# Hybrid decoder step on one core: in prompt attention TensorE does the value products and the turn back ahead of the next group's logits

## The chip, the core and the metric

The kernel runs on one core of a Trainium2 chip. The metric is the device time of one execution in microseconds (us), the median of several runs. Five engines work side by side, each through its own queue of instructions in program order, and meet by semaphores: TensorE (PE, its weight loads listed apart as PEld), VectorE (DVE), ScalarE (ACT), GpSimd (POOL) and SyncE (SP, which issues DMAs).

## What is computed

One decoder layer over a prompt of 2048 positions and a decode batch of 64 positions with a paged cache. Projection, forgetting attention and pooling, output mix and norm, then a convolutional feed-forward block with norm. The change touches only the prompt's attention, 8 heads of width 64, in float32:

```python
s = jnp.einsum('bqhd,bkhd->bhqk', q, k).astype(jnp.float32) * ATTN_SCALE
s = s + jnp.swapaxes(qc, 1, 2)[..., :, None] - jnp.swapaxes(kc, 1, 2)[..., None, :]
s = jnp.where(causal, s, NEG_INF)
p = jax.nn.softmax(s, axis=-1)
return jnp.einsum('bhqk,bkhd->bqhd', p.astype(v.dtype), v)
```

## The kernel before

The stages follow one another: `stage_project`, `stage_gates_pool`, `stage_attention`, `stage_mix_prompt`, then feed-forward with the decode batch's attention beside it. The prompt attention is `stage_attention`.

**Groups, steps and pairs.** The work is cut into 32 groups: a head and a block of 512 queries (four rows r of 128 queries). The blocks of a head are taken 0 to 3, those of the next head 3 to 0. Group g of a head sees 4g+4 blocks of 128 keys, and each of these is a step: 320 steps, done two at a time in 160 pairs. In this text p is a pair, and p-1 the one before it.

**What a pair holds.** Six kinds of work, with a letter for each that the prediction uses:

- T(p), TensorE, `transposes`, L912: the exponentials of the pair's two key blocks, up to 8 tiles of 128x128, are turned into a bank of `ps_t` for each step. There are four banks (TBANKS); a bank is free when DVE has read it (`t_free`).
- H(p), ACT, `high`, L1029: the rounded upper half of each bank goes to `p_hi`.
- R(p), DVE, `rest`, L977: what is left, bank minus `p_hi`, goes to `p_lo`, and frees the bank. DVE does R(p-1) in its turn of pair p.
- V(p), TensorE, `times_v`, L924 and L926: two products with the values for each step, summed in `ps_o`. V(p-1) is done in TensorE's turn of pair p, and waits for R(p-1) by `t_free`.
- L(p), TensorE, `logits`, L896, L897 and, where a piece has the diagonal, L900: pieces of up to 512 logits of the *next* group, in three banks of `ps_s` (SBANKS). A table, `logits_at`, spreads the 320 pieces over the pairs by columns: 115 pairs have some (one to eight pieces), 45 have none, those at the end of a group.
- C(p), DVE, `copy_logits`, L965 (with a small reduce, L969, after a row's last piece): scales the piece into `row`, takes its minimum and frees its bank.

Besides these ACT does the exponentials (`exp`, L1021) by the table `exps_at` and, at a group's end, copies `ps_o` out (`o_out`, L1035). In the second pair of the next group TensorE turns that copy back (`turn_back`, L936, four matmuls into a `ps_t` bank), and in the pair after it DVE normalises it (`normalise`, L984, L987, L994).

**What sets the order.** Each engine's program is written out by hand as a loop over pairs. TensorE's is T(p), L(p), V(p-1), turn back. DVE's is

```python
if 1 <= pair <= PAIRS:
    rest(i - 2)
    rest(i - 1)
for n in nat_at.get(pair - 1, []):
    normalise(n)
for n, r, j in logits_at.get(i, []) + logits_at.get(i + 1, []):
    copy_logits(n, r, j)
```

so it is R(p-1), the normalising where there is one, C(p). ACT's is H(p), the copy out, the exponentials. The numbers of `ps_t` banks (`tick_of`, `nat_tick`) are set by a loop of their own, which the change leaves alone.

Of the kernel before, what the change touches and what calls it, by code (L numbers as in the profile page):

```python
# [757 lines left out]
def stage_attention(nc, io, sc, persist):  # L758
    groups = [(h, g) for h in range(H) for g in (range(4) if h % 2 == 0 else reversed(range(4)))]
    NGR = len(groups)  # L760
    steps = [4 * g + 4 for _, g in groups]
    first_t = [sum(steps[:n]) for n in range(NGR + 1)]
    NTR = first_t[NGR]
# [10 lines left out]
    def pieces(n, r):  # L774
        return cut(n, r, PIECE)
# [20 lines left out]
    logits_at, exps_at = {}, {}  # L796
# [41 lines left out]
    with ExitStack() as ctx:  # L838
# [44 lines left out]
        def _(pe):  # L883
            def logits(n, r, j):
                h, g = groups[n]
                par, q = h % 2, 4 * g + r
                if n % 4 == 0 and r == 0:
                    pe.wait_ge(head_in[par], 128 * (h // 2 + 1))
                cols = slice(q * P, (q + 1) * P)
                o, w = pieces(n, r)[j]  # L890
                p = piece_of[n, r] + j
                if p >= SBANKS:
                    pe.wait_ge(s_copied, p - SBANKS + 1)
                out, keys = ps_s[:, p % SBANKS, 0:w], slice(o, o + w)
                diagonal = keys.stop == (q + 1) * P
                nc.tensor.matmul(out, qs[:, par, cols], ks[:, par, keys], start=True, stop=False, skip_group_check=True)  # L896
                last = nc.tensor.matmul(out, q2[:, par, cols], k2[:, par, keys], start=False, stop=not diagonal,  # L897
                                        skip_group_check=True)
                if diagonal:
                    last = nc.tensor.matmul(out[:, w - P:w], identb[:, :], causal[:, :], start=False, stop=True,  # L900
                                            skip_group_check=True)
                last.then_inc(s_done, 1)

            def transposes(i):
                n, k = turns[i]
                tk = tick_of[i]
                if k * P % HALF == 0:
                    pe.wait_ge(exp_done, exps_until(n, k * P // HALF))
                if tk >= TBANKS:
                    pe.wait_ge(t_free, tk - TBANKS + 1)  # L910
                for r in range(skip(i), 4):
                    last = nc.tensor.transpose(ps_t[:, tk % TBANKS, r * P:(r + 1) * P],  # L912
                                               row[:, n % 2, r, k * P:(k + 1) * P], ident[:, :])
                last.then_inc(t_done, 1)

            def times_v(i):
                n, k = turns[i]
                h, o = groups[n][0], skip(i) * P
                pe.wait_ge(t_free, tick_of[i] + 1)
                if n % 4 == 0 and k == 0:  # L920
                    pe.wait_ge(v_in[h % 2], 16 * (h // 2 + 1))
                if k == 0 and n:
                    pe.wait_ge(o_copied, n)
                nc.tensor.matmul(ps_o[:, o:512], v[:, h % 2, k, :], p_hi[:, i % PBUF, o:512], start=k == 0, stop=False,  # L924
                                 skip_group_check=True)
                nc.tensor.matmul(ps_o[:, o:512], v[:, h % 2, k, :], p_lo[:, i % PBUF, o:512], start=False,  # L926
                                 stop=k == steps[n] - 1, skip_group_check=True).then_inc(pv_done, 1)

            def turn_back(n):
                tk = nat_tick[n]  # L930
                if n == 0:
                    pe.wait_ge(c_in, 32)
                pe.wait_ge(o_copied, n + 1)
                pe.wait_ge(t_free, tk - TBANKS + 1)
                for r in range(4):
                    last = nc.tensor.matmul(ps_t[:, tk % TBANKS, r * HD:(r + 1) * HD], oT[:, n % 2, r * P:(r + 1) * P], both[:, :],  # L936
                                            start=True, stop=True)
                last.then_inc(nat_done, 1)
# [3 lines left out]
            for pair in range(PAIRS + 2):  # L942
                i = 2 * pair
                if pair < PAIRS:
                    transposes(i)
                    transposes(i + 1)
                    for n, r, j in logits_at.get(i, []) + logits_at.get(i + 1, []):
                        logits(n, r, j)
                if 1 <= pair <= PAIRS:
                    times_v(i - 2)  # L950
                    times_v(i - 1)
                for n in nat_at.get(pair, []):
                    turn_back(n)

        @block.vector
        def _(dve):
# [1691 lines left out]
```

## Time and profile before

| | us |
|---|---|
| median of 3 runs | 3067.35 |
| lowest and highest | 3066.34, 3074.68 |
| the profiled execution, its own time | 3075.47 |
| span of its trace | 3073.8 |
| attention stage in it, from 462 to 947 | 485.0 |

Over the whole span PE is busy 2939.5 us (96%), DVE 2009.4 (65%), ACT 1484.3 (48%), POOL 811.1 (26%). These are averages over stages with different limits; for the change the stage between 462 and 947 us is to be read by itself. The views print, for a stretch, each engine's busy time and the granted clock of TensorE (PEclk, 1.00 is 2.4 GHz and 0.50 is 1.2 GHz); in the timeline an instruction's start, its length, and in brackets how long its engine was idle before it and who released it. Lengths of matmuls hold a modelled end, so matmuls overlap in the list; the distance from start to start is what one costs TensorE.

### The profile page before, as it was taken

The numbers are of one execution on the slowest core, as the hardware profiler recorded it, in microseconds if no ns is written. First come the engines' busy times: TensorE is split into PE (matmuls) and PEld (weight loads), VectorE is DVE, ScalarE is ACT, GpSimd is POOL, SyncE is SP. The second block draws the span as 40 slices with busy tenths as digits, with TensorE's granted clock in tenths as the row PEclk, the third lists the DMA queues.
The fourth block names the chain that finished last, engine by engine and source line by source line (L and its number), as shares of the span: only waits on it lengthen the run. The fifth ranks groups of instructions, "written<-read, shape, count | busy, mean of one in ns | idle before, by whom it ended". The sixth has DMA issues, their size and how long they took to land. (4 is left out here: it accounts for less than half of the span.)

```text
span 3073.8 us, 56650 instructions
## 1 busy us (share of the span) xinstructions
PE 2939.5 (96%) x19248; PEld 2367.9 (77%) x19248; DVE 2009.4 (65%) x4190; ACT 1484.3 (48%) x3057; POOL 811.1 (26%) x1437
## 2 busy tenths in 40 slices
PE   7999968999998997999999999999999999999997
PEld 7999957777777885877777777777777777777762
DVE  5433447787786656866678667678667668666454
ACT  3111115676674213466445656445665435666424
POOL 1110010000000103534445333455344353342300
PEclk9999978999999998999999999999999999999999
DMA  5444465224203447767979677888677886775877
GB/s 208 137 138 123 117 170 129 70 56 97 77 1 131 131 144 241 254 202 241 310 258 314 225 238 246 282 300 296 212 254 241 273 302 226 250 250 169 288 273 322
DMA packets 271943, 629.62 MB, mean 205 GB/s; under 512 B 53400, under 2 KB 117816, under 8 KB 263680
## 3 DMA queue, kind: packets, MB, share of 16 engines
q1 hardware_dynamic: 171095, 308.46, 31.4%
q0 software_dynamic: 93760, 296.83, 29.1%
q10 hardware_dynamic: 6800, 20.71, 2.1%
q8 instruction: 154, 2.52, 0.3%
q14 instruction: 134, 1.09, 0.1%
HBM read 558.66 MB, written 67.33 MB: 204 GB/s over the span
## 5 line engine op out<-in xcount | busy, mean ns | idle before, releaser
L1615 PE MATMUL F_ps_u<-X_x_hi,F_w_hi 128*128 128x512 f32 x1408 | 572.9, 407 | 7.0 <-DVE F_w_lo L1879 7.0
L1616 PE MATMUL F_ps_u<-X_x_lo,F_w_hi 128*128 128x512 f32 x1408 | 560.3, 398 | 0.0
L1617 PE MATMUL F_ps_u<-X_x_hi,F_w_lo 128*128 128x512 f32 x1408 | 560.1, 398 | 0.0
L2157 POOL DMA_DIRECT2D N_dec<-cache_v x512 | 282.0, 551 | 618.9 <-PE F_ps_d L1679 484.7
L1879 DVE TENSOR_TENSOR F_w_lo<-X_raw,F_w_hi 128x512 fp32r<-128x512 f32 x352 | 238.1, 678 | 239.5 <-ACT F_w_hi L1777 238.4
L2117 POOL DMA_DIRECT2D N_dec<-cache_k x512 | 278.1, 543 | 338.5 <-issue 188.3
L1938 DVE STREAM_TRANSPOSE N_dec<-N_dec 128x1024 f32<-128x1024 f32 x256 | 310.5, 1230 | 49.2 <-DMA N_dec<-cache_k 49.2
L1777 ACT CAST F_w_hi<-X_raw 128x512 fp32r<-128x512 f32 x352 | 215.7, 613 | 251.9 <-PE F_ps_y L1617 200.4
L1615 PEld LDWEIGHTS F_ps_u<-X_x_hi,F_w_hi 128*128 128x128 f32 x1408 | 266.8, 190 | 85.5 <-issue 19.2
L1617 PEld LDWEIGHTS F_ps_u<-X_x_hi,F_w_lo 128*128 128x128 f32 x1408 | 266.4, 189 | 64.6
L1616 PEld LDWEIGHTS F_ps_u<-X_x_lo,F_w_hi 128*128 128x128 f32 x1408 | 267.1, 190 | 58.7
L1802 ACT ACTIVATE F_h<-F_ps_u,F_coef 128x512 f32<-128x512 f32 x176 | 121.2, 689 | 372.8 <-PE F_ps_u L1617 371.0
L965 DVE TENSOR_SCALAR_CACHE_REDUCE C_row<-C_ps_s 128x512 f32<-128x512 f32 (+2 forms) x320 | 185.6, 608 | 83.7 <-PE C_ps_s L897 61.2
L254 PE MATMUL A_ps_p<-A_w_hi,A_x_hi 128*128 128x412 f32 x600 | 210.7, 351 | 0.0
L256 PE MATMUL A_ps_p<-A_w_hi,A_x_lo 128*128 128x412 f32 x600 | 209.7, 349 | 0.0
L255 PE MATMUL A_ps_p<-A_w_lo,A_x_hi 128*128 128x412 f32 x600 | 209.5, 349 | 0.0
L1330 POOL TENSOR_TENSOR H_qs<-Dp_pin,H_qs 128x512 fp32r<-128x512 f32 x16 | 23.2, 1452 | 683.1 <-ACT H_qs L1242 683.1
L1879 DVE TENSOR_TENSOR F_w_lo<-F_raw,F_w_hi 128x512 fp32r<-128x512 f32 x176 | 118.8, 676 | 124.0 <-ACT F_w_hi L1777 123.6
L1615 PE MATMUL F_ps_y<-F_w_hi,F_g_hi 128*128 128x512 f32 x480 | 195.5, 407 | 3.4 <-DVE F_g_lo L1891 2.2
L1029 ACT CAST C_p_hi<-C_ps_t 128x512 fp32r<-128x512 f32 (+1 forms) x320 | 151.7, 527 | 91.8 <-PE C_ps_t L912 91.7
L1617 PE MATMUL F_ps_y<-F_w_hi,F_g_lo 128*128 128x512 f32 x480 | 190.1, 396 | 0.0
L1616 PE MATMUL F_ps_y<-F_w_lo,F_g_hi 128*128 128x512 f32 x480 | 189.4, 395 | 0.0
(349 smaller groups left out, 6226.4 us busy)
## 6 DMA issues: line engine op xcount, KB each, us to landing
N_dec<-cache_k POOLq DMA_DIRECT2D x512, 256.0 KB, 4.8
N_dec<-cache_v POOLq DMA_DIRECT2D x512, 256.0 KB, 4.2
X_raw<-w_up_t SPq DMA_DIRECT2D x120, 512.0 KB, 5.8
F_raw<-w_up_t SPq DMA_DIRECT2D x56, 512.0 KB, 5.7
X_raw<-w_down SPq DMA_DIRECT2D x56, 512.0 KB, 5.6
sc_qk<-A_early SPq DMA_DIRECT2D x16, 1024.0 KB, 5.1
F_forget<-sc_wT POOLq DMA_DIRECT2D x256, 64.0 KB, 5.2
F_raw<-w_down SPq DMA_DIRECT2D x32, 512.0 KB, 5.4
```

The costliest lines, as they stand in the source:

```text
L254: nc.tensor.matmul(out, x_hi[:, t % 2, c, :], w_hi[:, c, cols], start=c == 0, stop=False)
L255: nc.tensor.matmul(out, x_hi[:, t % 2, c, :], w_lo[:, c, cols], start=False, stop=False)
L256: last = nc.tensor.matmul(out, x_lo[:, t % 2, c, :], w_hi[:, c, cols], start=False, stop=c == DC - 1)
L965: nc.vector.tensor_scalar(row[:, n % 2, r, o:o + w], ps_s[:, p % SBANKS, 0:w], -SCALE, None, ALU.mult, ALU.min, accum_out=least[:, n % 4, ...
L1615: nc.tensor.matmul(out, a_hi, b_hi, start=first, stop=False)
L1616: nc.tensor.matmul(out, a_hi, b_lo, start=False, stop=False)
L1617: return nc.tensor.matmul(out, a_lo, b_hi, start=False, stop=last)
L1777: nc.scalar.copy(w_hi[:, q % 4, :], raw[unit % RAW][:, q % 2 * 512:(q % 2 + 1) * 512]).then_inc(hi_done, 1)
L1879: nc.vector.tensor_tensor(w_lo[:, q % 4, :], raw[q // 2 % RAW][:, q % 2 * 512:(q % 2 + 1) * 512], w_hi[:, q % 4, :].bitcast(F32), ALU.subt ...
L1938: nc.vector.transpose(kt[n % 2][:, :, half % 2 * 64:(half % 2 + 1) * 64].rearrange("p f (j t) -> p j f t", j=2), kin[:, half % KR, :, :].r ...
L2117: pool.dma_start(kin[:, half % KR, j, :], io["cache_k"][ds(pages[j], 1), :, :].rearrange("a t c -> (a t) c"))\
L2157: pool.dma_start(vin[j:P:4, n % 2, :, :], io["cache_v"][ds(pages[j], 1), :, :].rearrange("a (b t) c -> (a t) b c", b=4))\
```

## The change

In TensorE's loop the logits of a pair move from between T(p) and V(p-1) to behind V(p-1) and the turn back. Nothing else changes: the programs of DVE, ACT, POOL and SP are the same, row for row.

```diff
                 if pair < PAIRS:
                     transposes(i)
                     transposes(i + 1)
-                    for n, r, j in logits_at.get(i, []) + logits_at.get(i + 1, []):
-                        logits(n, r, j)
                 if 1 <= pair <= PAIRS:
                     times_v(i - 2)
                     times_v(i - 1)
                 for n in nat_at.get(pair, []):
                     turn_back(n)
+                for n, r, j in logits_at.get(i, []) + logits_at.get(i + 1, []):
+                    logits(n, r, j)
```

In the three places below each row is one instruction (with a count where it repeats), output<-inputs and the output's shape: `C_ps_t` is written by T (L912) and by the turn back (L936), `C_ps_s` by L, `C_ps_o` by V. All three are TensorE's rows in the fourth group (head 0, its fourth block of queries).

**In the middle of the group**, its third pair p. Before, the five matmuls of L(p) stand between T(p) and V(p-1):

```order
L912 MATMUL C_ps_t<-all_ident,C_row 128x128 x8
L896 MATMUL C_ps_s<-H_ks,H_qs 128x512
L897 MATMUL C_ps_s<-X_x_lo,X_x_hi 128x512
L896 MATMUL C_ps_s<-H_ks,H_qs 128x256
L897 MATMUL C_ps_s<-X_x_lo,X_x_hi 128x256
L900 MATMUL C_ps_s<-all_masks 128x128
L924 MATMUL C_ps_o<-C_p_hi,C_v 128x512
L926 MATMUL C_ps_o<-C_p_lo,C_v 128x512
L924 MATMUL C_ps_o<-C_p_hi,C_v 128x512
L926 MATMUL C_ps_o<-C_p_lo,C_v 128x512
L912 MATMUL C_ps_t<-all_ident,C_row 128x128 x8
```

Now they stand behind V(p-1):

```order
L912 MATMUL C_ps_t<-all_ident,C_row 128x128 x8
L924 MATMUL C_ps_o<-C_p_hi,C_v 128x512
L926 MATMUL C_ps_o<-C_p_lo,C_v 128x512
L924 MATMUL C_ps_o<-C_p_hi,C_v 128x512
L926 MATMUL C_ps_o<-C_p_lo,C_v 128x512
L896 MATMUL C_ps_s<-H_ks,H_qs 128x512
L897 MATMUL C_ps_s<-X_x_lo,X_x_hi 128x512
L896 MATMUL C_ps_s<-H_ks,H_qs 128x256
L897 MATMUL C_ps_s<-X_x_lo,X_x_hi 128x256
L900 MATMUL C_ps_s<-all_masks 128x128
L912 MATMUL C_ps_t<-all_ident,C_row 128x128 x8
```

The four matmuls of V(p-1), which wait for DVE's R(p-1), are now ahead of the logits for which DVE's C(p) waits. Of the 115 pairs with logits, 84 follow a pair that had some too, as here: these are called middle pairs in the prediction.

**With a turn back**, the second pair of the group. Before:

```order
L896 MATMUL C_ps_s<-H_ks,H_qs 128x128
L897 MATMUL C_ps_s<-X_x_lo,X_x_hi 128x128
L900 MATMUL C_ps_s<-all_masks 128x128
L896 MATMUL C_ps_s<-H_ks,H_qs 128x512
L897 MATMUL C_ps_s<-X_x_lo,X_x_hi 128x512
L896 MATMUL C_ps_s<-H_ks,H_qs 128x512
L897 MATMUL C_ps_s<-X_x_lo,X_x_hi 128x512
L924 MATMUL C_ps_o<-C_p_hi,C_v 128x512
L926 MATMUL C_ps_o<-C_p_lo,C_v 128x512
L924 MATMUL C_ps_o<-C_p_hi,C_v 128x512
L926 MATMUL C_ps_o<-C_p_lo,C_v 128x512
L936 MATMUL C_ps_t<-C_both,X_raw 128x64 x4
```

Now:

```order
L924 MATMUL C_ps_o<-C_p_hi,C_v 128x512
L926 MATMUL C_ps_o<-C_p_lo,C_v 128x512
L924 MATMUL C_ps_o<-C_p_hi,C_v 128x512
L926 MATMUL C_ps_o<-C_p_lo,C_v 128x512
L936 MATMUL C_ps_t<-C_both,X_raw 128x64 x4
L896 MATMUL C_ps_s<-H_ks,H_qs 128x128
L897 MATMUL C_ps_s<-X_x_lo,X_x_hi 128x128
L900 MATMUL C_ps_s<-all_masks 128x128
L896 MATMUL C_ps_s<-H_ks,H_qs 128x512
L897 MATMUL C_ps_s<-X_x_lo,X_x_hi 128x512
L896 MATMUL C_ps_s<-H_ks,H_qs 128x512
L897 MATMUL C_ps_s<-X_x_lo,X_x_hi 128x512
```

The four matmuls of the turn back are ahead of the logits too. There are 32 of these pairs, and 24 of them are middle pairs; of the 32 pairs behind them, in which DVE normalises, 20 are middle pairs.

**At the start of a group**, its first pair. Before:

```order
L912 MATMUL C_ps_t<-all_ident,C_row 128x128 x8
L896 MATMUL C_ps_s<-H_ks,H_qs 128x512
L897 MATMUL C_ps_s<-X_x_lo,X_x_hi 128x512
L896 MATMUL C_ps_s<-H_ks,H_qs 128x512
L897 MATMUL C_ps_s<-X_x_lo,X_x_hi 128x512
L896 MATMUL C_ps_s<-H_ks,H_qs 128x512
L897 MATMUL C_ps_s<-X_x_lo,X_x_hi 128x512
L924 MATMUL C_ps_o<-C_p_hi,C_v 128x256
L926 MATMUL C_ps_o<-C_p_lo,C_v 128x256
L924 MATMUL C_ps_o<-C_p_hi,C_v 128x128
L926 MATMUL C_ps_o<-C_p_lo,C_v 128x128
L912 MATMUL C_ps_t<-all_ident,C_row 128x128 x8
```

Now:

```order
L912 MATMUL C_ps_t<-all_ident,C_row 128x128 x8
L924 MATMUL C_ps_o<-C_p_hi,C_v 128x256
L926 MATMUL C_ps_o<-C_p_lo,C_v 128x256
L924 MATMUL C_ps_o<-C_p_hi,C_v 128x128
L926 MATMUL C_ps_o<-C_p_lo,C_v 128x128
L896 MATMUL C_ps_s<-H_ks,H_qs 128x512
L897 MATMUL C_ps_s<-X_x_lo,X_x_hi 128x512
L896 MATMUL C_ps_s<-H_ks,H_qs 128x512
L897 MATMUL C_ps_s<-X_x_lo,X_x_hi 128x512
L896 MATMUL C_ps_s<-H_ks,H_qs 128x512
L897 MATMUL C_ps_s<-X_x_lo,X_x_hi 128x512
L912 MATMUL C_ps_t<-all_ident,C_row 128x128 x8
```

Here V(p-1) is narrow, since it belongs to the diagonal's last two key blocks. There are 31 such first pairs with a pair without logits before them; the very first pair of all has no V(p-1) and does not change.

## Rows read from the trace of the kernel before

**Rows 1.** Busy time by stretch: length, PE, PEld, DVE, ACT, POOL, then PEclk

```profile
462.00:947.00 485.00, 456.14 (x2752) 371.17 (x2752) 385.67 (x1135) 333.11 (x736) 0.00 (x0) 0.97 0.28 67
```

**Rows 2.** Waits between 462 and 947 us: total us, times, longest

```profile
DVE C_row L965 <- PE C_ps_s L897: 61.2, 55, 4.9
...
PEld C_ps_o L924 <- DVE C_p_lo L977: 28.9, 72, 1.8
DVE C_row L965 <- PE C_ps_s L900: 20.4, 22, 5.8
...
PE C_ps_t L912 <- ACT C_row L1021: 13.4, 20, 1.8
```

**Rows 3.** Timeline, one middle pair: start, length, engine, line, instruction

```profile
548.03 1.03 PE L912 MATMUL C_ps_t<-all_ident,C_row 128*128 128x128 f32 x8
...
548.40 1.28 DVE L977 TENSOR_TENSOR C_p_lo<-C_ps_t,C_p_hi 128x512 fp32r<-128x512 f32 x2
...
548.82 0.47 PE L896 MATMUL C_ps_s<-H_ks,H_qs 128*128 128x512 f32 x1
...
549.69 0.69 DVE L965 TENSOR_SCALAR_CACHE_REDUCE C_row<-C_ps_s 128x512 f32<-128x512 f32 x1
...
550.30 1.28 DVE L977 TENSOR_TENSOR C_p_lo<-C_ps_t,C_p_hi 128x512 fp32r<-128x512 f32 x2
```

**Rows 4.** Timeline, a group's start and a pair with a turn back

```profile
561.30 0.28 PE L924 MATMUL C_ps_o<-C_p_hi,C_v 128*128 128x256 f32 x1
...
561.71 1.06 PE L912 MATMUL C_ps_t<-all_ident,C_row 128*128 128x128 f32 x8
...
562.55 1.28 DVE L977 TENSOR_TENSOR C_p_lo<-C_ps_t,C_p_hi 128x512 fp32r<-128x512 f32 x2
...
563.75 0.41 DVE L965 TENSOR_SCALAR_CACHE_REDUCE C_row<-C_ps_s 128x256 f32<-128x256 f32 x1
...
563.91 0.47 PE L924 MATMUL C_ps_o<-C_p_hi,C_v 128*128 128x512 f32 x1
...
564.46 1.00 PE L936 MATMUL C_ps_t<-C_both,X_raw 128*128 128x64 f32 x8
...
565.29 1.06 PE L912 MATMUL C_ps_t<-all_ident,C_row 128*128 128x128 f32 x8
```

**Rows 5.** Timeline, the next two pairs: DVE's normalising, then logits

```profile
566.15 0.15 DVE L984 TENSOR_TENSOR C_total<-C_total 128x4 f32<-128x4 f32 x1
...
566.96 0.55 DVE L965 TENSOR_SCALAR_CACHE_REDUCE C_row<-C_ps_s 128x384 f32<-128x384 f32 x1
...
568.39 0.47 PE L896 MATMUL C_ps_s<-H_ks,H_qs 128*128 128x512 f32 x1
...
568.70 0.39 PE L897 MATMUL C_ps_s<-X_x_lo,X_x_hi 68*128 68x512 f32 x1
...
568.93 0.40 PE L896 MATMUL C_ps_s<-H_ks,H_qs 128*128 128x512 f32 x1
...
569.25 0.69 DVE L965 TENSOR_SCALAR_CACHE_REDUCE C_row<-C_ps_s 128x512 f32<-128x512 f32 x1 [0.33 <-PE C_ps_s L897]
```

**Rows 6.** Timeline, DVE at the start of a group with large blocks

```profile
518.33 0.69 DVE L965 TENSOR_SCALAR_CACHE_REDUCE C_row<-C_ps_s 128x512 f32<-128x512 f32 x1 [2.10 <-PE C_ps_s L897]
```

**Rows 7.** Busy time by stretch, columns as in the first group

```profile
468.00:470.00 2.00, 2.00 (x9) 1.81 (x7) 0.07 (x1) 1.07 (x2) 0.00 (x0) 0.50 0.99 381
...
592.00:596.00 4.00, 3.00 (x16) 1.73 (x15) 3.89 (x16) 1.31 (x4) 0.00 (x0) 1.00 0.49 92
596.00:600.00 4.00, 2.27 (x15) 1.97 (x16) 1.58 (x6) 3.60 (x8) 0.00 (x0) 1.00 0.60 244
600.00:604.00 4.00, 4.00 (x17) 3.38 (x16) 1.77 (x7) 1.07 (x2) 0.00 (x0) 0.57 0.00 0
```

**Rows 8.** Timeline, logits early in the stage, at the lower clock

```profile
468.69 0.78 PE L896 MATMUL C_ps_s<-H_ks,H_qs 128*128 128x512 f32 x1
...
469.93 0.69 DVE L965 TENSOR_SCALAR_CACHE_REDUCE C_row<-C_ps_s 128x512 f32<-128x512 f32 x1 [3.55 <-PE C_ps_s L897]
```

## The prediction, made before the changed kernel ran

> **What bounds the kernel now.** I read the averages by stretch first, then the list of waits, then the timeline of single pairs. The attention stage takes 485.0 us. PE is busy 456.1 of them and DVE 385.7 [rows 1], which looks like a PE-bound stage. But PE's busy time holds the modelled ends of its matmuls, and the list of waits says who waits for whom: DVE waits for logits in 61.2 + 20.4 = 81.6 us, 77 times, and PE's weight loads wait for DVE's R 72 times, 28.9 us in all, 0.4 us each [rows 2]. So both run near their limit and push each other. The timeline tells where DVE's 81.6 us lie. Counted there, 43 of the 77 waits are shorter than 1 us, like the 0.33 us before 569.25 [rows 5], and come to 10.6 us; nearly all of the rest, 71 us, stand at a group's start, like the 2.10 us of [rows 6], when the first logits of a new group must wait for its first transposes. In the middle of a group DVE hardly waits at all: R(p-1) from 548.40, C(p) at 549.69, the next R at 550.30, without a gap [rows 3].
>
> Why it doesn't wait there is the point. PE issues T(p) at 548.03 and the first matmul of L(p) at 548.82, while DVE is still in R(p-1) (548.40 to 549.68). When R(p-1) ends, the logits stand ready in `ps_s`, and C(p) starts at once [rows 3]. V(p-1), which needs R(p-1), is done by PE while DVE is in C(p). The two engines overlap because L(p) asks for nothing that DVE does in this pair.
>
> **The change, part by part.** No instruction is added or removed, and only PE's program moves. But L(p) is now queued on PE behind V(p-1), which waits for DVE's R(p-1); and DVE's next work in order is C(p), which waits for L(p). So DVE must idle from the end of R(p-1) until PE has got through what is left of V(p-1) and the first piece of L(p). Nothing else can fill it: behind C(p) on DVE stands R(p), in program order, and behind that everything.
>
> *Middle pairs (84).* From the end of R(p-1) to the end of V(p-1)'s issue: R ends at 562.55 + 1.28 = 563.83, V's second half starts at 563.91, and what PE has next starts at 564.46 [rows 4]: 0.63 us. (V's first half runs during R's second half, so only the second counts.) From the first matmul of L to the start of C: 568.39 to 569.25, 0.86 us [rows 5]; of this 0.08 us goes away, since behind V its second matmul follows after 0.23 us (568.70 to 568.93) and not after 0.31 (568.39 to 568.70). That is 0.63 + 0.78 = 1.41 us. Today C starts even 0.08 us before the modelled end of R (563.75 against 563.83), so C comes 1.49 us later. 84 x 1.49 = 125 us. Off this go the short waits of today, 10.6 us, and about 3 us because in 32 of these pairs the first piece is narrower than 512. Comes to **+111 us**. I see no way round it: the number of `ps_s` banks doesn't help, as DVE has emptied all three when it goes into R(p-1).
>
> *Turn back (24 middle pairs).* Its matmuls are now ahead of the logits as well: 564.46 to 565.29, 0.83 us [rows 4], which nothing hides. 24 x 0.83 = **+20 us**. In the pair after it the turn back holds one `ps_t` bank, so the second step of T(p) waits for the first half of R(p-1), then costs PE about 0.4 us, half of the T from 548.03 to 548.82 [rows 3], before V(p-1) can start. V's second half would have had to wait for R's second half anyway; some 0.3 us stay, in 20 middle pairs: **+6 us**.
>
> *Normalising (20 middle pairs).* It lies between R(p-1) and C(p) on DVE, 566.15 to 566.96, 0.81 us [rows 5]. Today it is on DVE's path, afterwards it falls into the new idle time: 20 x 0.81 = **-16 us**.
>
> *Starts of groups (31).* There R(p-1) has long been done when T(p) ends, so only V(p-1)'s own time comes in before the logits, and it is narrow: 561.30 to 561.71, 0.41 us [rows 4]. 31 x 0.41 = **+13 us**.
>
> *Exponentials.* PE waits for them 13.4 us in 20 waits, before a group's first transposes [rows 2]. ACT's other work gets more room in longer pairs, and T of a pair without logits comes directly behind L now, so H is done sooner. I take -4 us, between 0 (nothing gained) and -13 (all of it). The copy out of `ps_o` comes earlier and was waited for by nobody; it is costed at nothing, and if it were late, it would cost the turn back no more than its own 0.83 us.
>
> *Sum.* 111 + 20 + 6 - 16 + 13 - 4 = **+130 us**. The stage goes from 485 to about 615 us, the profiled execution from 3075.5 to about 3205 us. That execution is 8.1 us above the median of 3067.35, so the median goes to 3067 + 130 = **3197 us**. The other stages issue the same instructions and begin later, and I cost them at nothing.
>
> **TensorE's clock.** It is the one resource that can make this worse. In a middle pair PE has T (548.03 to 548.82, 0.8 us), V (four matmuls at 0.23, the spacing from 568.70 to 568.93 [rows 5], 0.9 us) and on average 2.3 pieces of L (192 pieces in 84 pairs) at 2 x 0.23, 1.1 us: 2.8 us. DVE's round is 1.2 (R, 562.55 to 563.75 [rows 4]) + 1.5 + 2.3 x 0.61 (C, 549.69 to 550.30 [rows 3]) + about 0.2 for the reduce, 4.3 us. So PE falls to about two thirds busy, with a gap of 1.4 us in each pair. The trace has such a stretch: between 592 and 596 us PE was busy 3.00 of 4 us and the granted clock stayed at 1.00, the 2.4 GHz level; between 596 and 600 it was busy 2.27 of 4 us, much of it in narrow matmuls, and the four microseconds after that ran at 0.57, mostly the 1.2 GHz level [rows 7]. PE two thirds busy lies between these two; as its gaps are short and its matmuls wide, I place the new middle pairs nearer to the first. The Trainium skill ("TensorE: Matmul & The Clock Gate", section "A second HAM failure mode: psum-queue depth-cycling") speaks against this change here: it says that micro-idles of PE between groups of matmuls, while PSUM banks are cycled, were enough to make the clock go back and forth between its two levels. By that rule the time would be that of the third rival below; by the row from 592 us it would be the forecast.
>
> **The rivals.**
>
> *1. Forecast, DVE idles in each pair.* For it: [rows 3], the program order on both engines, and DVE's missing slack in the middle of a group. Nothing in the trace speaks against it; only the size is open.
>
> *2. Faster.* The value products no longer stand behind the logits, so their banks, the copy out and the turn back come earlier. At the groups with eight pieces in one pair this could shorten the chain into the exponentials. At most it gives back what PE and its loads wait for, 28.9 + 13.4 = 42 us [rows 2]: 3025 us. It decides only if the new idle per middle pair is under 42/84 = 0.5 us, a third of what the rows give, that is, if PE took logits ahead of a waiting V(p-1). Chance 0.03.
>
> *3. The clock falls in the middle of groups.* At the lower clock (0.50 between 468 and 470 us [rows 7]) first logits to C takes 468.69 to 469.93, 1.24 us, in place of 0.86 [rows 8], and matmul issue doubles: PE's 2.8 us become 5.6, above DVE's round of 4.3, so PE sets the pair and 5.6 - 4.3 = 1.3 us come on top. If it holds for half of the 84 pairs, 55 us more, 3252 us; for all, 109 us, 3306 us. Chance 0.10.
>
> *4. No change.* The 1.49 us are hidden because other engines set the pair: then ACT, busy 333.1 of 485 us [rows 1], would have to be the bound, but it leaves 152 us. 3067 us. Chance 0.03.
>
> *5. The same mechanism, smaller.* Waits of today fall into the new gap more than I counted (turn back beside the reduce, ACT's waits): without the turn back and with 1.2 us in place of 1.49 it is 130 - 20 - 24 = +86 us, 3153 us. Chance 0.10; the forecast keeps 0.74.
>
> **How the numbers follow.** Low end 3160: the sum with 1.3 us in place of 1.49 per middle pair (-16), all 13 us of the exponentials' waits gone (-9) and half of the turn back hidden (-10) is +95, 3162. High end 3242: the sum and a low clock in 35 of the middle pairs, 35 x 1.3 = 45 us. Left out are rivals 2 and 4, the low part of 5, and the high part of 3. A difference under 0.3% (9 us) can't be told from no change here. Faster by more 0.03, within 0.03, slower by more 0.94.
>
> **What would show it.** In the changed kernel's profile: the stage lasts near 615 us with DVE's busy time still near 386, so its idle time goes from 99 to about 230 us; the wait of C for L grows from 81.6 us in 77 waits to about 210 in some 115, with one of about 1.4 us in each middle pair, about 2.2 with a turn back (0.4 at most above today's at a group's start); the wait of V for R goes from 28.9 us to over 100; the exponentials' wait is no longer than 13.4 us; PEclk in the stage stays at 0.95 or above. Wrong would be: middle pairs in which DVE starts C within 0.5 us of R's end (then 2 or 4), or PEclk under 0.9 over the stage (then 3), or ACT's exponentials as the releaser in most pairs, which I have not costed.

## The result, and the profile after

The changed kernel takes 3191.78 us in the median (3190.21 to 3193.00), the kernel before, run beside it, 3067.82 us (3066.34 to 3074.68). The ratio is 1.0400, with a 95% interval of 1.0387 to 1.0414: slower by 124 us, where 130 us were predicted. Its profiled execution took 3192.42 us and is the one read below. The page first, of the changed kernel: span, busy time of each engine, and from the costliest groups those of C and of V (busy time and ns of one, then idle time before them and what ended most of it):

```profile
span 3190.8 us, 56650 instructions
...
PE 2966.0 (93%) x19248; PEld 2366.5 (74%) x19248; DVE 2011.1 (63%) x4190; ACT 1491.1 (47%) x3057; POOL 811.2 (25%) x1437
...
L965 DVE TENSOR_SCALAR_CACHE_REDUCE C_row<-C_ps_s 128x512 f32<-128x512 f32 (+2 forms) x320 | 185.9, 609 | 208.5 <-PE C_ps_s L897 109.3
...
L924 PE MATMUL C_ps_o<-C_p_hi,C_v 128*128 128x512 f32 (+1 forms) x320 | 138.9, 438 | 88.6 <-DVE C_p_lo L977 88.1
```

Nothing was added to any engine's work: DVE is busy 2011.1 us against 2009.4 before, over the whole span. The stage, from the first logits to the end of attention, shows it better (length, PE, PEld, DVE, ACT, POOL, then PEclk, the granted clock):

```profile
460.70:1071.30 610.60, 485.66 (x2752) 372.43 (x2752) 387.81 (x1136) 339.85 (x736) 0.00 (x0) 0.96 0.22 54
```

Against [rows 1] the stage is 125.6 us longer with DVE's busy time 2 us more, so DVE's idle time went from 99.3 to 222.8 us. (The window of [rows 1] ends just before DVE's last normalising, 947.13 to 947.56. From the first logits to the end of the last normalising the stage took 485.35 us before and 610.38 now, 125.0 us more.) PE's busy time, in which overlaps count once, rose by 29.5 us with the same 2752 instructions at nearly the same clock. Most of that is not work: added up one by one, the lengths of these instructions grew by 11 us only (909.7 to 920.9). A modelled end that overlapped the next matmul before now stands in a pause. So the 93% of PE on the page say little; the list of waits says more (us in total, times, longest), changed kernel, 460 to 1072 us:

```profile
ACT C_p_hi L1029 <- PE C_ps_t L912: 260.7, 167, 6.5
PEld C_ps_o L924 <- DVE C_p_lo L977: 136.1, 188, 2.0
DVE C_row L965 <- PE C_ps_s L897: 109.3, 72, 6.2
DVE C_row L965 <- PE C_ps_s L900: 97.9, 57, 6.8
...
PE C_ps_t L912 <- DVE C_p_lo L977: 29.0, 24, 1.4
...
PE C_ps_t L912 <- ACT C_row L1021: 4.8, 4, 1.6
```

DVE's wait for logits is 109.3 + 97.9 = 207.2 us in 129 waits, against 61.2 + 20.4 = 81.6 in 77 [rows 2]. The growth, 125.6 us, is that of the stage to within 1 us. V's wait for R went from 28.9 to 136.1 us (the weight loads' wait). A new kind is T waiting for R, 29.0 us in 24 waits. ACT's long waits cost nothing: it has work for 340 of 611 us.

Where DVE waits is seen in the timeline (start, length, engine, line, instruction, and in brackets the idle time before it and its releaser). A plain middle pair of the changed kernel, to be laid beside [rows 3]:

```profile
594.92 1.29 DVE L977 TENSOR_TENSOR C_p_lo<-C_ps_t,C_p_hi 128x512 fp32r<-128x512 f32 x2
...
595.67 0.51 PE L924 MATMUL C_ps_o<-C_p_hi,C_v 128*128 128x512 f32 x1 [0.70 <-DVE C_p_lo L977]
...
596.26 0.50 PE L924 MATMUL C_ps_o<-C_p_hi,C_v 128*128 128x512 f32 x1
...
596.83 0.39 PE L896 MATMUL C_ps_s<-H_ks,H_qs 128*128 128x512 f32 x1
...
597.62 0.69 DVE L965 TENSOR_SCALAR_CACHE_REDUCE C_row<-C_ps_s 128x512 f32<-128x512 f32 x1 [1.41 <-PE C_ps_s L897]
```

R(p-1) runs from 594.92 to 596.21. V's first half starts when R's first half is done, V's second half when the second is, and only at 596.83 does PE come to the logits. DVE stands still from 596.21 to 597.62, 1.41 us. In [rows 3] the logits were started at 548.82, in the middle of R, and C followed R without a gap.

A pair with a turn back, changed kernel: the turn back (four matmuls in the program, which the profile lists as eight) lies between V and L as well, and the gap is 2.15 us.

```profile
588.03 0.50 PE L924 MATMUL C_ps_o<-C_p_hi,C_v 128*128 128x512 f32 x1
...
588.60 1.00 PE L936 MATMUL C_ps_t<-C_both,X_raw 128*128 128x64 f32 x8
...
589.41 0.36 PE L896 MATMUL C_ps_s<-H_ks,H_qs 128*128 128x256 f32 x1
...
590.12 0.42 DVE L965 TENSOR_SCALAR_CACHE_REDUCE C_row<-C_ps_s 128x256 f32<-128x256 f32 x1 [2.15 <-PE C_ps_s L900]
```

The pair after it: T's second step has to wait for a `ps_t` bank until R's first half has read it; normalising (here its last part) stands in what would have been DVE's gap, of which 0.81 us stay.

```profile
591.33 1.28 DVE L977 TENSOR_TENSOR C_p_lo<-C_ps_t,C_p_hi 128x512 fp32r<-128x512 f32 x2
...
592.08 0.66 PE L912 MATMUL C_ps_t<-all_ident,C_row 128*128 128x128 f32 x4 [1.15 <-DVE C_p_lo L977]
...
593.00 0.42 DVE L994 TENSOR_TENSOR CD_att<-C_ps_t,C_rec 128x256 f32<-128x256 f32 x1
...
593.03 0.40 PE L924 MATMUL C_ps_o<-C_p_hi,C_v 128*128 128x512 f32 x1
...
594.24 0.56 DVE L965 TENSOR_SCALAR_CACHE_REDUCE C_row<-C_ps_s 128x384 f32<-128x384 f32 x1 [0.81 <-PE C_ps_s L900]
```

Here V's second half (593.03) starts 0.42 us behind R's end (592.61) and not 0.05 us as at 596.26, since T's second step stood ahead of V.

The same count was made over the whole stage from DVE's timeline: its idle times of over 0.15 us before the first copy of a pair, in us, by kind of pair, for the kernels of this study. (The four copies before the first pair, some 7 us, and the very first pair, 3.55 us, are in the list of waits and not here, nor are later copies of a pair. That leaves 30 starts of groups in which V(p-1) can stand ahead of logits.)

| DVE's wait for a pair's first copy | before | changed | e1 | e3 | e6 | e2 | e12 | e11 |
|---|---|---|---|---|---|---|---|---|
| 40 plain middle pairs | 5.5 | 56.5 | 56.5 | 32.5 | 5.5 | 5.4 | 5.5 | 3.4 |
| 24 middle pairs with turn back | 2.1 | 53.2 | 31.8 | 18.3 | 30.9 | 1.4 | 4.4 | 3.2 |
| 20 middle pairs with normalising | 2.2 | 19.3 | 17.9 | 8.8 | 0.0 | 2.2 | 4.6 | 25.9 |
| 30 starts of groups | 59.5 | 64.2 | 67.4 | 60.9 | 63.6 | 71.2 | 14.7 | 82.6 |

The middle pairs wait 129.0 us in place of 9.8, the starts 64.2 in place of 59.5: together 123.9 us, which is the loss to within 1 us.

### The profile page after: what moved, and what is told of

Same layout as the page of the kernel before. It is cut to its first block and busy times, and to the rows that moved or that the text cites. A ratio compares the mean times of both kernels' runs of the same rounds, so it can differ in the third digit from the quotient of the medians.

```text
span 3190.8 us, 56650 instructions
## 1 busy us (share of the span) xinstructions
PE 2966.0 (93%) x19248; PEld 2366.5 (74%) x19248; DVE 2011.1 (63%) x4190; ACT 1491.1 (47%) x3057; POOL 811.2 (25%) x1437
## 5 line engine op out<-in xcount | busy, mean ns | idle before, releaser
L965 DVE TENSOR_SCALAR_CACHE_REDUCE C_row<-C_ps_s 128x512 f32<-128x512 f32 (+2 forms) x320 | 185.9, 609 | 208.5 <-PE C_ps_s L897 109.3
L924 PE MATMUL C_ps_o<-C_p_hi,C_v 128*128 128x512 f32 (+1 forms) x320 | 138.9, 438 | 88.6 <-DVE C_p_lo L977 88.1
```

The costliest lines, as they stand in the source:

```text
L965: nc.vector.tensor_scalar(row[:, n % 2, r, o:o + w], ps_s[:, p % SBANKS, 0:w], -SCALE, None, ALU.mult, ALU.min, accum_out=least[:, n % 4, ...
```

## The experiments

The theory: what costs is not PE's order as such but a closed circle of two program orders. On PE, L(p) stands behind V(p-1), which waits for R(p-1); on DVE, C(p) stands behind R(p-1) and waits for L(p). Each engine then idles while the other works. Rivals were that the loss lies in the clock or in PE's pauses, in banks, or in some other step of the pair. All times below are medians; the kernel before had 3068 to 3069 us beside them.

### One part alone: the turn back, the starts, a half

**e1_turn_back_behind** keeps V ahead of L, but puts the turn back behind the logits again.

```diff
-                for n in nat_at.get(pair, []):
-                    turn_back(n)
                 for n, r, j in logits_at.get(i, []) + logits_at.get(i + 1, []):
                     logits(n, r, j)
+                for n in nat_at.get(pair, []):
+                    turn_back(n)
```

> TensorE's order in a pair is T, V, L, turn back: the value products stay ahead of the logits, the turn back goes behind them again. Theory (DVE idles from the end of R until PE has done what is queued ahead of L): the 24 middle pairs with a turn back wait for logits 1.4 us like the others and no longer 2.15 us, so 24 x 0.75 = 18 us less than the changed kernel, about 3174 us. Rival (the turn back runs while DVE is busy anyway and the whole loss is the value products'): 3192 us, no difference to the changed kernel.

Measured: 3172.02 us, ratio 1.0337 (1.0320 to 1.0354). Being ahead of the logits costs the turn back 3191.8 - 3172.0 = 20 us, as the sum had it (24 x 0.83). The table shows where: pairs with a turn back wait 31.8 us in place of 53.2, a median of 1.26 us in place of 2.15, and the pairs behind them 17.9 in place of 19.3. That last difference, 1.4 us, comes from one pair of the changed kernel at a low clock (see the clock below). It doesn't price the bank that the turn back holds, since in e1 the turn back holds it too: T waits for R 24 times there as well, 8.3 us in all. Everything else, 103 us, is V ahead of L.

**e2_starts_only** is the kernel before with V ahead of L only in the first pair of a group; all other pairs are as before.

```diff
-                    for n, r, j in logits_at.get(i, []) + logits_at.get(i + 1, []):
-                        logits(n, r, j)
+                    new = i in first_t
+                    if not new:
+                        for n, r, j in logits_at.get(i, []) + logits_at.get(i + 1, []):
+                            logits(n, r, j)
                 if 1 <= pair <= PAIRS:
                     times_v(i - 2)
                     times_v(i - 1)
+                if pair < PAIRS and new:
+                    for n, r, j in logits_at.get(i, []) + logits_at.get(i + 1, []):
+                        logits(n, r, j)
```

> The value products go ahead of the logits only in the first pair of each group (31 pairs that have a V); the turn back and all other pairs stand as in the kernel before. The prediction's term for these pairs is +13 us (31 x 0.41), 3081 us. The changed kernel's trace has 5 us more of waits for logits in the 30 of them that the trace tells apart, and PE waits 8.6 us less for exponentials; if these belong to the first pairs alone, 3073 us. Rival (the first pairs carry much of the loss, since each new group waits for them): 3100 us or more.

Measured: 3081.27 us, ratio 1.0037 (1.0023 to 1.0051), so +12 us, and the starts wait 71.2 us in place of 59.5. The term of 13 us is right. The pairs that it concerns are 30 and not 31: the very first pair has no V, and the last group no logits behind it. They lose 0.4 us each and not 1.4, since R is done there: in e2's trace V's second half starts 0.69 us or more behind R's end in each of the 30. V ahead of L is cheap where V waits for nothing.

**e3_between** is the changed kernel with L between the two halves of V, so that the turn back is behind L again.

```diff
                 if 1 <= pair <= PAIRS:
                     times_v(i - 2)
+                for n, r, j in logits_at.get(i, []) + logits_at.get(i + 1, []):
+                    logits(n, r, j)
+                if 1 <= pair <= PAIRS:
                     times_v(i - 1)
...
-                for n, r, j in logits_at.get(i, []) + logits_at.get(i + 1, []):
-                    logits(n, r, j)
```

> TensorE's order is T, first half of V, L, second half of V, turn back. Theory: the first half of V waits only for the first half of R, so L is issued while DVE is in the second half of R. By the changed kernel's rows: first half of V starts 0.06 us after the first half of R, takes 0.57 us, first logits to C 0.78 us, so C starts 1.41 us after the first half of R ends, of which the second half of R covers 0.6 us: about 0.8 us idle per middle pair in place of 1.41. 84 x 0.6 = 50 us less, and 18 us less as the turn back is behind L: 3124 us. Rival (what costs is only that L stands behind any product, or that V is early, not how long DVE waits): 3174 us, as with the turn back alone put back.

Measured: 3120.33 us, ratio 1.0159 (1.0139 to 1.0180). L now hangs on R's first half alone, and the gap of a plain middle pair goes from 1.41 to 0.81 us in the median. The whole loss is 51 us, where e1, which has the turn back behind L too, had 103. Its stage (columns as above):

```profile
460.50:998.80 538.30, 476.35 (x2752) 378.54 (x2752) 388.07 (x1136) 337.29 (x736) 0.00 (x0) 0.96 0.25 61
```

The clock is that of the changed kernel, 0.96; it is DVE's gaps that have changed.

### Opening the circle on DVE's side

**e4_copies_late** is the changed kernel on PE, word for word, with one edit on DVE: in a pair it does the copies of the pair before, behind R, so that it no longer waits for logits that hang on this very R.

```diff
                     rest(i - 2)
                     rest(i - 1)
+                for n, r, j in logits_at.get(i - 2, []) + logits_at.get(i - 1, []):
+                    copy_logits(n, r, j)
                 for n in nat_at.get(pair - 1, []):
                     normalise(n)
-                for n, r, j in logits_at.get(i, []) + logits_at.get(i + 1, []):
-                    copy_logits(n, r, j)
```

> The changed kernel with one edit on DVE: it copies the logits of the pair before (which PE issued a whole T and V earlier) in place of this pair's, and normalises behind them. PE's order is that of the changed kernel. Theory: the loss is DVE's wait for logits queued behind products that wait for DVE itself; with the copies a pair later that circle is open, the waits of about 1.4 us are gone in middle pairs, and the time falls to about that of the kernel before, 3045 to 3085 us; the exponentials come later and may cost 20 us of it. Rival (PE's own order costs, because it stands idle for R before it can do the logits, whatever DVE does): 3170 to 3192 us.

Measured: 3077.66 us, ratio 1.0031 (1.0021 to 1.0041). Of the 124 us lost, 114 come back, with PE's new order and the number of banks kept. This is the strongest evidence for the circle. What the copies' delay costs in turn is in the waits of this kernel: the rows come late to the exponentials, T to ACT, H to R.

```profile
DVE C_p_lo L977 <- ACT C_p_hi L1029: 71.7, 55, 5.2
...
PE C_ps_t L912 <- ACT C_row L1021: 34.0, 20, 3.3
DVE C_row L965 <- PE C_ps_s L900: 19.7, 20, 7.0
...
PEld C_ps_o L924 <- DVE C_p_lo L977: 5.1, 19, 0.8
...
DVE C_row L965 <- PE C_ps_s L897: 4.7, 14, 0.9
```

Waits for logits are down to 24.4 us and V's wait for R to 5.1, but R waits 71.7 us for H and T 34.0 us for exponentials.

**e5_before_copies_late** has the same late copies with the kernel before's order on PE.

```diff
                     rest(i - 2)
                     rest(i - 1)
+                for n, r, j in logits_at.get(i - 2, []) + logits_at.get(i - 1, []):
+                    copy_logits(n, r, j)
                 for n in nat_at.get(pair - 1, []):
                     normalise(n)
-                for n, r, j in logits_at.get(i, []) + logits_at.get(i + 1, []):
-                    copy_logits(n, r, j)
```

> The kernel before (T, L, V on TensorE) with DVE's copies one pair late, as in the run with late copies: the two differ only in the order that the change is about. Theory: that order costs only because DVE's next work hangs on the logits in the same pair; with late copies it does not, so both orders are within 10 us of each other, 3068 to 3088 us. Rival (the new order costs or gains something of its own on TensorE): more than 20 us apart.

Measured: 3097.29 us, ratio 1.0091 (1.0074 to 1.0108). This missed: 19.6 us above e4, where at most 10 were expected. With late copies the changed order is the better one. Waits of e5, 460 to 980 us:

```profile
DVE C_p_lo L977 <- ACT C_p_hi L1029: 101.1, 103, 5.2
...
PEld C_ps_s L896 <- DVE C_row L965: 41.1, 57, 2.1
...
PE C_ps_s L896 <- DVE C_row L965: 22.0, 34, 1.7
```

If DVE empties the `ps_s` banks only behind R, then L, in front of V on PE, waits for banks (22.0 us in 34 waits on PE; 3.3 us in e4), and V and the next T stand behind it. Read so, it is the circle with the parts exchanged: the step whose input comes last on the other engine must stand last. That is taken from the waits and was not tested by itself; R's wait for H grew as well, from 71.7 us in e4 to 101.1.

**e8_late_early5** and **e9_before_early5** ask whether e4's late exponentials can be made good by computing logits two steps earlier, with `EARLY` 5 in place of 3, on top of e4 and of the kernel before.

```diff
-    EARLY, EXP_AFTER = 3, 2
+    EARLY, EXP_AFTER = 5, 2
```

> The changed order with late copies, and EARLY 5 in place of 3, so that a group's last logits are made one pair earlier. In the run with late copies TensorE waited 34 us for exponentials in 20 waits at the starts of groups, against 13.4 us in the kernel before, since copies and exponentials come a pair later. Theory: with one pair more these waits mostly go, 20 to 30 us: about 3052 us, which would beat the kernel before. Rival (the waits only change place, as DVE has the same work in fewer pairs and R waits for it): 3070 to 3080 us.

> The kernel before with EARLY 5 alone, to tell that number's own effect from that of the late copies. TensorE waits 13.4 us for exponentials in the kernel before; at best these go, 3055 us. More likely the fuller pairs cost DVE what the group's start gains: 3062 to 3075 us.

Measured: e8 3073.63 us, ratio 1.0011 (0.9998 to 1.0024), e9 3067.06 us, ratio 0.9992 (0.9980 to 1.0003). e9 came out as expected; e8 missed its 3052 us and fell to its rival. In e8 T's wait for exponentials falls from 34.0 to 16.6 us, but R still waits 71.0 us for H and V now 15.8 us for R. So the order of the changed kernel can be had at no loss, and I found no form in which it gains.

### Which step may stand ahead of the logits

**e6_turn_back_first** is the kernel before with T, turn back, L, V: only the turn back ahead of the logits, which needs nothing of this pair's R. Expected was next to no loss.

```diff
+                for n in nat_at.get(pair, []):
+                    turn_back(n)
...
-                for n in nat_at.get(pair, []):
-                    turn_back(n)
```

> Only the turn back goes ahead: TensorE's order is T, turn back, L, V. Theory: while the value products stay behind the logits, the logits still wait for nothing that DVE does in this pair; the turn back's 0.83 us are issued while DVE is in R (1.2 us), so of 24 x 0.83 = 20 us most is hidden: 3069 to 3078 us. Rival (the turn back costs its 20 us wherever it stands ahead of the logits): 3088 us.

Measured: 3093.28 us, ratio 1.0078 (1.0061 to 1.0094), a miss of 15 us and more; the rival's 3088 us was nearer. The timeline of e6 at a pair with a turn back:

```profile
692.60 1.28 DVE L977 TENSOR_TENSOR C_p_lo<-C_ps_t,C_p_hi 128x512 fp32r<-128x512 f32 x2
...
693.43 1.08 PE L936 MATMUL C_ps_t<-C_both,X_raw 128*128 128x64 f32 x8 [0.95 <-DVE C_p_lo L977]
...
694.32 0.36 PE L896 MATMUL C_ps_s<-H_ks,H_qs 128*128 128x256 f32 x1
...
695.03 0.42 DVE L965 TENSOR_SCALAR_CACHE_REDUCE C_row<-C_ps_s 128x256 f32<-128x256 f32 x1 [1.15 <-PE C_ps_s L900]
```

The turn back reads nothing of R, but it writes into a `ps_t` bank, and the four are taken until R(p-1)'s first half has read one. It waits 0.95 us for that, and behind it the logits: the same circle, closed by a free bank and not by data. The other thing that it needs, ACT's copy out of `ps_o`, had ended 0.38 to 1.23 us before the turn back began in all 24 middle pairs, whereas in 22 of them it began 0.15 us behind the end of R's first half, as here. It came to 30.9 - 2.1 = 28.8 us of waits in 24 pairs, less 2.2 us gained at the normalising; the starts wait 4.1 us more. e1's +103 us and e6's +25 us make 128 us, near the 124 us of the whole change, but that doesn't show that its two parts add up: in the changed kernel the turn back stands behind V, has no wait for R left, and costs its own 0.83 us.

The list of waits of e6 puts its weight loads' wait down to ACT's copy (20.6 us in 28 waits) and its matmuls' to R. **e11_turn_back_later** is e6 with `NAT_AFTER` 3 in place of 2, a pair later, to see whether e6's wait was for ACT's copy out of `ps_o` and would be gone by then.

```diff
-    PAIRS, NAT_AFTER = NTR // 2, 2
+    PAIRS, NAT_AFTER = NTR // 2, 3
```

> As the run with the turn back alone ahead of the logits (which took 3093 us, and in which the turn back's weight loads waited 20.6 us in 28 waits for ACT's copy of the sums), but a pair later (NAT_AFTER 3), when the copy is long done. Theory: the 25 us of that run were its wait for ACT plus its own 0.83 us, less what R covers; without the wait, 0.83 us against the slack of R: at most 10 us are left, 3068 to 3080 us. Rival (0.83 us cost DVE their full length ahead of the logits, wait or no wait): 3088 us.

Measured: 3105.12 us, ratio 1.0117 (1.0100 to 1.0134), worse than e6 and 25 us and more above what was expected. The wait has only moved one pair on, to the 20 middle pairs that were those with normalising, 25.9 us, and its releaser in the trace of e11 is still R:

```profile
548.07 1.29 DVE L977 TENSOR_TENSOR C_p_lo<-C_ps_t,C_p_hi 128x512 fp32r<-128x512 f32 x2
...
548.90 1.07 PE L936 MATMUL C_ps_t<-C_both,X_raw 128*128 128x64 f32 x8 [0.24 <-DVE C_p_lo L977]
...
550.67 0.69 DVE L965 TENSOR_SCALAR_CACHE_REDUCE C_row<-C_ps_s 128x512 f32<-128x512 f32 x1 [1.31 <-PE C_ps_s L897]
```

So in e6 it is the bank. Of the starts, six (those of the first two groups of the third, fifth and seventh head) wait 39.9 us in e11 and 15.5 before. Why is left open; T waits 19.2 us for exponentials there, and the execution that was profiled was the slowest of its four, 3117.70 us, with PEclk 0.90 in the stage.

**e7_one_ahead** has only the first piece of L ahead of V, the others behind V and the turn back (the edit is shown against the kernel before). If the first copy's cover were enough, this would cost nothing.

```diff
-                    for n, r, j in logits_at.get(i, []) + logits_at.get(i + 1, []):
+                    for n, r, j in (logits_at.get(i, []) + logits_at.get(i + 1, []))[:1]:
                         logits(n, r, j)
...
+                for n, r, j in (logits_at.get(i, []) + logits_at.get(i + 1, []))[1:]:
+                    logits(n, r, j)
```

> The changed kernel, but the first piece of a pair's logits stands ahead of V again; the other pieces stay behind V and the turn back. Theory: DVE starts C at once, and waits for the second piece instead, which comes 1.41 us after R's end (2.15 with a turn back) while the first copy covers about 0.55 us. Of the 84 middle pairs 64 have a second piece: 28 plain ones x 0.85, 20 with a turn back x 1.6, 16 with normalising x 0.1, together 58 us, and the 20 with one piece cost nothing: 3123 us. Rival (only the start of C matters, and one copy is cover enough): 3068 to 3080 us.

Measured: 3136.67 us, ratio 1.0225 (1.0208 to 1.0242). The gap moves from the first copy to the second: 4.4 us in all before the first copies of the 84 middle pairs, and before the second ones 21.8 us in 28 plain pairs (0.78 each), 36.4 in 20 with a turn back (1.82) and 10.9 in 16 with normalising (0.68). One copy of 0.6 us covers 0.6 us of the gap and no more. The size was missed by 14 us: 9 at the pairs with normalising, for which 0.1 each had been worked out, and 4 at those with a turn back (1.6). The former come behind a turn back, and T waits in them for the `ps_t` bank that it holds:

```profile
PE C_ps_t L912 <- DVE C_p_lo L979: 24.8, 20, 1.5
```

It costs more here than in the changed kernel (some 0.25 us a pair, see below). From R's first half on T's second step (0.4 us), the first piece (0.46), V (0.93) and the second piece (0.78) come one after the other, 2.6 us, and normalising and the first copy end 0.81 + 0.6 us behind R, which is 2.05 us behind R's first half. That is a reckoning from durations of the trace; it gives 0.5 us of the 0.68 found, and was not tested by itself.

### The other way round

**e12_start_logits_first.** Before and after, DVE's largest waits were at the starts of groups, 59.5 us, where T stands ahead of L and waits for exponentials. There L depends on nothing of T. This kernel is the one before, with up to three pieces of L (as many as there are banks) ahead of T in a group's first pair: the opposite of the change, made where there is room for it.

```diff
+                    new = logits_at.get(i, []) + logits_at.get(i + 1, [])
+                    ahead = SBANKS if i in first_t and pair else 0
+                    for n, r, j in new[:ahead]:
+                        logits(n, r, j)
                     transposes(i)
                     transposes(i + 1)
-                    for n, r, j in logits_at.get(i, []) + logits_at.get(i + 1, []):
+                    for n, r, j in new[ahead:]:
                         logits(n, r, j)
```

> The change turned round: in the kernel before, up to three pieces of logits of a group's first pair go ahead even of its transposes; all other pairs are as before. In the kernel before DVE waits 59.5 us for logits in the 30 such pairs, about 2 us each, as the logits stand behind transposes that wait for exponentials. Theory: they come 0.8 us and the exponentials' wait (13.4 us in all) earlier, H and R stay hidden behind the copies: 20 to 30 us less, about 3045 us, faster than both kernels. Rival (the transposes now come later by the logits' 1.4 us, and R waits for H instead): 3065 to 3085 us.

Measured: 3043.34 us (3039.79 to 3045.22), ratio 0.9916 (0.9899 to 0.9933), 25 us faster than the kernel before and 148 us faster than the changed one. Its stage and, from its list of waits, C's and T's (C is on line 969 there, the exponentials on 1025):

```profile
461.20:921.00 459.80, 441.89 (x2752) 366.99 (x2752) 389.34 (x1136) 330.82 (x736) 0.00 (x0) 0.98 0.29 71
```

```profile
DVE C_row L969 <- PE C_ps_s L897: 26.4, 55, 3.5
DVE C_row L969 <- PE C_ps_s L900: 19.3, 42, 5.7
...
PE C_ps_t L912 <- ACT C_row L1025: 3.0, 4, 1.6
```

The group start of [rows 6], in e12:

```profile
508.90 0.39 PE L896 MATMUL C_ps_s<-H_ks,H_qs 128*128 128x512 f32 x1
...
509.68 0.69 DVE L969 TENSOR_SCALAR_CACHE_REDUCE C_row<-C_ps_s 128x512 f32<-128x512 f32 x1 [0.77 <-PE C_ps_s L897]
...
510.31 1.04 PE L912 MATMUL C_ps_t<-all_ident,C_row 128*128 128x128 f32 x8
```

DVE waits 0.77 us where it waited 2.10. The starts' waits fall from 59.5 to 14.7 us, and the stage is 25.2 us shorter. That 45 us of waits gave 25 us is because others grew, by 19 us together: before a start's fourth piece, the first that stands behind T, DVE waits 6.7 us in place of 0.6; the middle pairs wait 5 us more; R waits 8.7 in place of 5.4 us for H; normalising, counted to its last one, 9.9 in place of 8.4 for the turn back; and DVE's busy time, counted so too, is 389.3 in place of 386.1.

## Why the prediction was right, step by step

The forecast was its first case, 3197 us with a range of 3160 to 3242, and 3191.78 was measured. By its own terms, with what the runs showed for each. Counted is the time from the end of R (or of the normalising) to the start of C, an overlap of the two as less than nothing, so that DVE's 2 us more of busy time need no line of their own:

| term | predicted | measured | from |
|---|---|---|---|
| middle pairs | +111 | +108 | 56.5 plain and 31.8 with turn back (e1), 28.0 with normalising if C came there as in plain pairs, less 8.2 before |
| normalising | -16 | -15 | the 20 pairs with it, changed: 34.0 from R's end, 19.3 from the normalising's |
| turn back's own time | +20 | +21 | pairs with it, 53.2 changed less 31.8 in e1 |
| the bank that it holds | +6 | +5 | the 20 pairs behind it against plain ones of the same width, changed |
| low clock in one of these | 0 | +1 | the pair whose logits are copied at 662.57 |
| starts of groups, with the exponentials | 13 - 4 = +9 | +5 | waits at the starts, 64.2 less 59.5 |
| sum | +130 | +125 | stage +125.0, median +124 |

*Middle pairs.* The step holds in each part. A plain middle pair's gap was built from the end of R to the next thing on PE, 0.63 us, and from L's first matmul to C, 0.78 us: 1.41 us. Those of 594.92 and on show 0.62 (596.21 to 596.83) and 0.79 (596.83 to 597.62), and the median over the 40 is 1.41. That the waits in the kernel before had to be taken off (10.6 us) was right too. Too large was the 0.08 us by which C was said to start before R's end: it was taken from one pair [rows 4], while [rows 3] has C at 549.69 behind R's end at 549.68, and over all 84 pairs of the kernel before these overlaps come to 2.6 us, not 84 x 0.08 = 6.7. e3 halves it by making L depend on half of R, e4 takes it away by making C independent of L(p), and neither changes what PE does in sum. That settles the cause.

*Turn back.* Predicted 2.2 us for such pairs; 2.15 in the median. The prediction's second part, some 0.3 us in each of the 20 pairs that follow, is borne out too: T does wait for the bank (24 times, 29.0 us), V's second half starts 0.41 us behind R's end in the median and not 0.06 as in plain pairs, and C comes 1.66 us behind R's end where a plain pair of that width has 1.41 (1.62 and 1.37 at width 384). That is 0.25 us a pair, 5 us in all. No run takes the bank's wait away by itself.

*Starts and exponentials.* In e2, which has the change at the starts alone, these wait 11.7 us more and the time is 12 us longer: the 13 us are about right (12.3 with the 30 pairs that there are). In the changed kernel the starts wait only 4.7 us more. At the same time T's wait for the exponentials, which stands before these very logits, is 4.8 us in place of 13.4 (9.4 in e2), 8.6 us less, where 4 of a possible 13 had been taken. The prediction's reason, that longer pairs leave ACT more time, agrees with e1 and e3, whose pairs are longer too and whose waits are 5.6 and 5.7 us; it was not tested by itself. This term, 4 us off, and the overlap in the middle pairs are the two that were mis-sized, and they make up most of the 5 us between forecast and result.

*Clock.* The stage's PEclk was 0.96 against 0.97, so the third rival (the clock falls in the middle of groups, 3252 us or more) did not come about, but for one middle pair: between 660 and 662 us the granted clock was 0.50, matmuls 128x512 started 0.42 us apart and not 0.23, and C came 3.03 us behind R's end in place of 1.66, about the 1.3 us that this rival put on a pair. Neither did the second and the fourth; the fifth, the same mechanism smaller, would have had 1.2 us a pair and a hidden turn back, and both were as the rows said.

*What was to be seen.* Stage near 615 us: 610.6. DVE's idle time about 230: 223. C's wait for L about 210 us in 115 waits: 207.2 in 129. V's wait for R over 100: 136.1. Exponentials' wait no longer than 13.4: 4.8. PEclk 0.95 or above: 0.96.

## What to carry to other kernels

Before moving a step on one engine, write down for both engines what stands behind what in program order, and close the loop: if A (here V) waits for the other engine's R, and L is put behind A, ask what the other engine does next after R. If that is what L feeds, both engines will take turns, and the price is the distance from the end of R to the first result of L, each time. It can be read from the trace before the change is made. A step that reads nothing late can still close the circle by the buffer it writes into (e6), and the order that is right on one engine depends on that of the other (e4 and e5). The place to gain is where a step with no late input stands behind one that waits: put it ahead there (e12).

## What the hardware showed that was not expected

One thing. The prediction gave one chance in ten to a falling clock, among other things because a stretch with PE busy 2.27 of 4 us was followed by one at 0.57 [rows 7]. The changed kernel has a pause of PE in each middle pair, and the granted clock stays at its upper level, 2.4 GHz, through nearly all of them. Busy times of the changed kernel by stretch (columns as above):

```profile
540.00:560.00 20.00, 15.18 (x86) 11.30 (x85) 12.80 (x34) 9.63 (x20) 0.00 (x0) 1.00 0.08 23
```

```profile
924.00:928.00 4.00, 2.39 (x12) 1.27 (x12) 3.93 (x14) 2.46 (x7) 0.00 (x0) 1.00 0.94 297
928.00:932.00 4.00, 3.18 (x20) 3.00 (x19) 0.67 (x3) 2.55 (x5) 0.00 (x0) 0.62 0.26 102
932.00:936.00 4.00, 4.00 (x14) 3.38 (x14) 1.76 (x7) 1.17 (x2) 0.00 (x0) 0.50 0.00 0
```

Of the 30 stretches of 20 us from 460 to 1060 us, 23 had a clock of 1.00 with PE busy for 14.85 to 17.04 us; in the kernel before the stretch from 540 us had PE busy for 19.95 us, at the same clock. Four more had 0.93 to 0.98, among them that of the pair at 662.57. In the stretch from 920 us (0.74) the clock fell behind a stretch in which PE had done little (2.39 of 4 us busy at 924, then 0.62 and 0.50), as in [rows 7]. It was also low at the stage's start (0.50 and 0.78 in the first two stretches of 20 us, 0.67 and 0.80 in the kernel before). The Trainium skill ("TensorE: Matmul & The Clock Gate", section "A second HAM failure mode: psum-queue depth-cycling") says of another kernel, in bf16, that frequent short idles of PE between groups of matmuls, while PSUM banks were cycled, made the clock swing between its two levels. With idle times of PE of 0.70 to 1.15 us in the pairs shown above that did not happen here from pair to pair: the stage's clock was 0.96.
